# Summing the modulation products over column tiles and turning them on TensorE

## The reference, cut to what matters

```python
def _modulation(cond, w, b):
    m = jax.nn.silu(cond) @ w + b
    return jnp.split(m, 3, axis=-1)

for i in range(DEPTH):                      # DEPTH = 4
    shift, scale, gate = _modulation(c, ada_w[i], ada_b[i])
    hx = _rmsnorm(x, norm_g[i]) * (1.0 + scale[:, None]) + shift[:, None]
    if kind == 1 or update_ctx:             # layers 0 and 1: the context stream too
        cshift, cscale, cgate = _modulation(c_ctx, ada_w[i], ada_b[i])
    ...                                     # pool, neighbourhood attention, conv, pool mixer
    x = x + gate[:, None] * yx
```

## Time and profile before

| | |
|---|---|
| median of 3 runs | 1907.27 us (1906.62 to 1909.27) |
| the profiled execution | 1906.62 us, of which the traced span is 1904.7 us |
| PE busy | 1881.4 us, 99% of the span |
| PEld, DVE, ACT, POOL busy | 82%, 31%, 48%, 72% |
| granted TensorE clock, mean | 0.999 of full speed |

### The profile page before, as it was taken

The page is one execution under the profiler, slowest core; times in us unless marked ns, Lnnn a source line. Parts: engine busy times, 40 slices in busy tenths (PEclk is TensorE's granted clock), DMA queues, the critical chain, the costliest instruction groups (busy, mean ns, idle before and its releaser), DMA issues.

```text
span 1904.7 us, 27387 instructions
## 1 busy us (share of the span) xinstructions
PE 1881.4 (99%) x10810; PEld 1560.1 (82%) x10810; DVE 590.6 (31%) x1037; ACT 912.2 (48%) x1365; POOL 1362.3 (72%) x568
## 2 busy tenths in 40 slices
PE   6999999999999999999999999999999999999999
PEld 5888788887888888888788888888888878888887
DVE  4213522774652500235621400120022563041011
ACT  3224511765454643465554454454435555545442
POOL 2514443457777698878678898879887957898875
PEclk9999999999999999999999999999999999999999
DMA  9762675439748476556456566557655655556653
GB/s 359 250 218 67 205 256 196 120 104 310 268 159 298 152 233 194 177 178 184 136 161 189 176 198 190 179 164 238 201 177 167 192 150 155 187 157 211 195 178 121
DMA packets 194845, 364.09 MB, mean 191 GB/s; under 512 B 32260, under 2 KB 48372, under 8 KB 194164
## 3 DMA queue, kind: packets, MB, share of 16 engines
q1 hardware_dynamic: 191280, 351.72, 58.7%
q10 hardware_dynamic: 3460, 10.88, 1.7%
HBM read 361.50 MB, written 6.10 MB: 193 GB/s over the span
## 4 chain that ended last, share of the span: by engine, by line
PE 94%; DMA 3%; SPq 1%; ACT 1%; DVE 1%; ACTq 0%; issue 0%
PE ps L1140 27%; PE ps L1142 26%; PE ps L1141 26%; PE ps L1346 3%; DMA proj<-in_ada_w 2%; PE ps L1158 2%; PE ps L1820 1%; PE ps L1819 1%; PE ps L1818 1%; PE ps L1734 1%; PE ps L1178 1%; PE ps L1498 1%; PE ps L1469 1%; PE ps L1479 1%; PE ps L1779 1%; SPq L375 1%
## 5 line engine op out<-in xcount | busy, mean ns | idle before, releaser
L514 POOL TENSOR_TENSOR w_lo<-raw,w_hi 128x1024 fp32r<-128x1024 f32 x556 | 1343.4, 2450 | 496.8 <-ACT w_hi L552 496.6
L1140 PE MATMUL ps<-w_hi,xt_hi 128*128 128x512 f32 (+1 forms) x1952 | 759.3, 389 | 4.6 <-DVE xt_lo L1973 4.2
L1142 PE MATMUL ps<-w_hi,xt_lo 128*128 128x512 f32 (+1 forms) x1952 | 744.4, 381 | 0.0
L1141 PE MATMUL ps<-w_lo,xt_hi 128*128 128x512 f32 (+1 forms) x1952 | 743.8, 381 | 0.0
L552 ACT ACTIVATE w_hi<-raw 128x1024 fp32r<-128x1024 f32 x556 | 567.4, 1057 | 330.8 <-DMA raw<-in_ffn_w_up 98.8
L1140 PEld LDWEIGHTS ps<-w_hi,xt_hi 128*128 128x128 f32 x1952 | 367.6, 188 | 81.9 <-issue 12.5
L1142 PEld LDWEIGHTS ps<-w_hi,xt_lo 128*128 128x128 f32 x1952 | 367.3, 188 | 71.7
L1141 PEld LDWEIGHTS ps<-w_lo,xt_hi 128*128 128x128 f32 x1952 | 368.0, 189 | 65.7
L1140 PE MATMUL ps<-w_hi,xt_hi_ctx 128*128 128x512 f32 (+1 forms) x432 | 169.0, 391 | 0.2
L1142 PE MATMUL ps<-w_hi,xt_lo_ctx 128*128 128x512 f32 (+1 forms) x432 | 166.8, 386 | 0.0
L1141 PE MATMUL ps<-w_lo,xt_hi_ctx 128*128 128x512 f32 (+1 forms) x432 | 166.5, 385 | 0.0
(11 more groups left out here) (221 smaller groups left out, 1477.7 us busy)
## 6 DMA issues: line engine op xcount, KB each, us to landing
raw<-in_w_in SPq DMA_DIRECT2D x120, 512.0 KB, 3.7
raw<-in_ffn_w_gate SPq DMA_DIRECT2D x88, 512.0 KB, 3.8
raw<-in_ffn_w_up SPq DMA_DIRECT2D x88, 512.0 KB, 3.8
raw<-in_ffn_w_down SPq DMA_DIRECT2D x88, 512.0 KB, 3.5
pt<-in_ada_w SPq DMA_DIRECT2D x44, 512.0 KB, 5.8
raw<-in_pool_w_in SPq DMA_DIRECT2D x32, 512.0 KB, 8.3
raw<-in_na_w_in SPq DMA_DIRECT2D x32, 512.0 KB, 5.0
raw<-in_conv_w_in SPq DMA_DIRECT2D x32, 512.0 KB, 5.7
```

The costliest lines, as they stand in the source:

```text
L514: pool.tensor_tensor(w_lo[:, s, :], raw[:, s, :], w_hi[:, s, :].bitcast(F32), ALU.subtract).then_inc(lo_done, 1)
L1140: pe.matmul(o, h, hi, start=start, stop=False)
L1141: pe.matmul(o, h, lo, start=False, stop=False)
L1142: return pe.matmul(o, c, hi, start=False, stop=stop)
```

## The change

A matmul of the modulation now takes all 512 columns of a chunk at once. Chunk m writes partitions 32·(m % 4) to 32·(m % 4)+31 of the bank, so chunks 0 and 4 are added in the first column tile, 1 and 5 in the second, and so on: a piece is 8 matmuls of 512 columns where it was 32 of 128, and its bank holds four partial sums. DVE copies the whole bank to `ada_rows` (in `qt`) and signals `ada_copied`; PE transposes it in four 128x128 blocks back into the same bank (`ada_turn`, `ada_turned`); DVE adds the four partial sums with a reduction (`ada_sums`, `ada_summed`) and then the bias as before.

```diff
-        def ada_cols(a, dims):
-            return free(qt[:, 0:1, 0:1], dims, 16 * SEQ + (a % 2) * P)
+        ada_rows = free(qt[:, 0:1, 0:1], [[1, 512]], 16 * SEQ)
...
                     for c in range(2):
                         m = 2 * k + c
-                        for j in range(4):
-                            last = pe.matmul(ps[32 * j:32 * j + 32, bank, 0:P], cond[:, m, :],
-                                             free(ada_slot(k, a), [[P, 4], [1, 32]], c * 512 + 32 * j), start=m == 0, stop=m == KC - 1)
+                        p0 = (m % 4) * 32
+                        last = pe.matmul(ps[p0:p0 + 32, bank, :], cond[:, m, :], ada_slot(k, a)[:, c * 512:(c + 1) * 512],
+                                         start=m < 4, stop=m >= 4)
                     last.then_inc(ada_used, 1)
+            def ada_turn(a, bank):
+                pe.wait_ge(ada_copied, a + 1)
+                for q in range(4):
+                    last = pe.transpose(ps[:, bank, q * P:(q + 1) * P], ada_rows[:, q * P:(q + 1) * P], ident[:])
+                last.then_inc(ada_turned, 1)
...                                   # in one_block, ahead of the matmuls of tile t in group k
+                        late = len(tiles) == NT and k < 3
+                        if t == tiles[len(tiles) // 2]:
+                            if k in ada and not late:
+                                ada_turn(ada[k], bank)
+                            if k - 1 in ada and len(tiles) == NT:
+                                ada_turn(ada[k - 1], bank)
...                                   # in start()
                 ada_products(0, 0)
                 ada_products(1, 1)
+                ada_turn(0, 0)
                 turn_half(0, 0)
                 turn_half(1, 0)
+                ada_turn(1, 1)
                 pe.wait_ge(ada_read, 2)
...
                 part(1, 0)
+                ada_turn(2, 2)
                 part(1, 1)
                 ada_products(3, 3)
                 read_out(bank_of(0, 2))
                 part(2, 0)
+                ada_turn(3, 3)
                 part(2, 1)
...
             def ada_block(a, bank):
+                ada_copy(a, bank)
+                ada_sum(a, bank)
+
+            def ada_copy(a, bank):
+                dve.wait_ge(ada_used, 4 * a + 4)
+                dve.tensor_copy(ada_rows, ps[:, bank, :]).then_inc(ada_copied, 1)
+
+            def ada_sum(a, bank):
                 n, to = conditions(a), 4 * ADA_ORDER[a]
-                dve.wait_ge(ada_used, 4 * a + 4)
-                if a > 1:
-                    dve.wait_ge(ada_read, a - 1)
-                dve.transpose(ada_cols(a, [[1, P]]), ps[:, bank, 0:P]).then_inc(ada_turned, 1)
                 dve.wait_ge(ada_turned, a + 1)
-                dve.tensor_tensor(mods[:, to:to + 4, 0:n], ada_cols(a, [[32, 4], [1, n]]),
+                dve.tensor_reduce(ada_sums[:, :, 0:n], free(ps[:, bank, 0:1], [[P, 4], [1, n], [32, 4]]), AX.X,
+                                  ALU.add).then_inc(ada_summed, 1)
+                dve.wait_ge(ada_summed, a + 1)
+                dve.tensor_tensor(mods[:, to:to + 4, 0:n], ada_sums[:, :, 0:n],
                                   free(cols[:, 0:1], [[1, 4], [0, n]], C_ADAB + to), ALU.add).then_inc(ada_read, 1)
```

More of the change, by code:

```diff
@@ L192, in program @@
         cond = sb("cond", [P, KC, 32])
+        ada_sums = sb("ada_sums", [P, 4, 2])
         rope = sb("rope", [P, 2, NT, HD])
@@ L212, in program @@
         ada_in = [[sem(f"ada_in{u}{k}") for k in range(4)] for u in range(2)]
-        ada_used, ada_turned, ada_read = sem("ada_used"), sem("ada_turned"), sem("ada_read")
+        ada_used, ada_copied, ada_turned, ada_summed, ada_read = (
+            sem(x) for x in ("ada_used", "ada_copied", "ada_turned", "ada_summed", "ada_read"))
         hi_done = sem("hi_done")
@@ L2618, in _ @@
             normed("p0", 3)
-            ada_block(2, 2)
+            ada_copy(2, 2)
             full_units("p0", 2, (0,), *modulated(0))
+            ada_sum(2, 2)
             low_of_tile("p0", 2, 0, 4)
             full_units("p0", 3, (0,), *modulated(0))
-            ada_block(3, 3)
+            ada_copy(3, 3)
             low_of_tile("p0", 3, 0, 4)
+            ada_sum(3, 3)
             first_gains(1)
```

## The result

| | before | after |
|---|---|---|
| median | 1907.07 us of 4 runs (1906.62 to 1909.27) | 1918.85 us of 4 runs (1918.16 to 1920.13) |
| span of the profiled execution | 1904.7 us | 1916.1 us |

The ratio is 1.0062, with a 95% interval of 1.0049 to 1.0076: slower by 11.8 us. The forecast was 1918.0 us. The two profiles differ by 11.4 us. First the head of the page, part 1 for PE, and then PE's waits (us in total, times, longest), which answer to the earlier trace rows.

What follows compares the result with a forecast made beforehand. PE's stream was taken as the bound, busy 1881.4 of 1904.7 us. Terms 0 + 8.8 + 0.2 + 0.5 + 1.3 = 10.8 us on 1906.62 gave 1917.4, predicted as 1918.0 us; own range 1915 to 1922.5, 8-in-10 range 1914 to 1932.

Steps and rivals of the forecast that it cites:

- Products, 0: Modulation products on PE: 16 passes of 512 columns cost the same as 64 of 128, four tiles fully overlapping; 0 us.
- The partial overlap: Rival for the products: tiles overlap as if three of four worked, 0.6 us more a piece, 1932 us; chance 0.06.
- Turn, 20·0.44 = 8.8: Four transposes on PE for each of pieces 4 to 23, 0.44 us each with nothing hiding them; 8.8 us.
- Waits at k = 3, 0.2: Next block waits for DVE's sum and bias add behind the turn, in seven pieces; 0.2 us in all, between 0 and 2.8.
- at piece 21, 0.5: PE reaches the turn at 527.3 but DVE, busy with L2250, lets it go on at about 527.8; new wait of 0.5 us.
- Opening, 1.3: Kernel start: two matmuls of piece 2's last slice 0.44 us longer, plus two turns of 0.44; 1.3 us, 0.4 to 2.7.
- the anchor: Opening: the first large matmul's 1.2 us delay does not last, because PE waits at 30.50 for piece 2's last slice.
- Late slices, cancelling: Where a slice is late, the wait shrinks by up to 0.44 us and the last slice takes longer; taken to cancel.

Runs made afterwards that it cites:

- e10: The kernel before the change with the slices of pieces 19 and 20 issued one weight group earlier; 1906.85 us, ratio 0.9999.
- e6: The changed kernel with 24 idle transposes keeping PE busy before the first large matmul; 1918.74 us, ratio 1.0063.
- e7: The changed kernel without POOL's first wait (L523) and with 24 idle transposes on PE before the first large matmul; 1922.15 us, ratio 1.0079.
- e3: The changed kernel with neighbouring chunks on one column tile (chunk m in tile m // 2 instead of m % 4); 1922.75 us, ratio 1.0083.
- e8: The changed kernel with neighbouring chunks on one column tile, and slices of pieces 19 and 20 issued one weight group earlier; 1922.05 us, ratio 1.0079.
- e5: The changed kernel without POOL's first wait for DVE's first gains (L523); 1923.01 us, ratio 1.008.

## Why the prediction was right

The profiled span grew by 11.4 us, where the sum was 10.8.

- **Products, 0.** Right, to 0.014 us a piece. The net cost is 2.06 for 2.08 us in the trace, and the experiments without a turn and with one alone agree. The partial overlap is refuted here, where the four tiles had plain fp32 matmuls: the rule of the Trainium skill, "TensorE: Matmul & The Clock Gate", section "Measured speedup vs the span model", of 2.38 for three tiles at 512 columns, would have put the net cost at about 2.5, an estimate. Four groups of 0.43 us for sixteen passes are four tiles without loss.
- **Turn, 20·0.44 = 8.8.** Right in kind, small by a ninth: 20·0.493 = 9.9, because of the slower steps behind each. That is the term of the main cost that was mis-sized.
- **Waits at k = 3, 0.2, and at piece 21, 0.5.** Neither came. At piece 21 DVE is free and waits for PE: in the kernel before it was held by L2250 until 527.03, 4 us behind the products. The same line is L2277 now; it ends 1.5 us later than before, while the products come 10 us later (531.24 for 521.21). The chain of DVE work that ends with it begins at this line, before:

```profile
493.22 1.22 DVE L2228 TENSOR_TENSOR proj<-proj,ps 128x1024 f32<-128x1024 f32 x1 [7.84 <-PE ps L1142]
```

  and after, with its end and the copy:

```profile
503.23 1.22 DVE L2255 TENSOR_TENSOR proj<-proj,ps 128x1024 f32<-128x1024 f32 x1 [3.24 <-PE ps L1142]
...
527.34 1.23 DVE L2277 TENSOR_TENSOR proj<-proj 128x1024 f32<-128x1024 f32 x1
533.25 0.69 DVE L1915 COPY qt<-ps 128x512 f32<-128x512 f32 x1 [4.68 <-PE ps L1158]
```

  So the chain began 10.0 us later, just as PE's stream did, and it was right to set DVE's time from before against PE's time from before. What changed is its length: 25.3 us for 33.9 (493.22 to 527.10). The time of its instructions depends on what POOL does beside them: four of L2241 took 8.40 us from 498.04 in the kernel before, and four of the same line, L2268 now, 1.80 us from 522.90 and from 525.51 in the kernel after, while POOL stood still from 522.4 to 527.96. This length is not a property of the change: it is 25.3 us in e10, which has the code of the kernel before, and 31.1 in e6 and 33.3 in e7, which have the stream of the kernel after. With 33.9 us the copy would have ended at 537.8 and PE, which is at the turn at about 537.4, would have waited some 0.4 us. That the term came out at nothing is luck.
- **Opening, 1.3.** Too small: it is 2.4 us at the large matmul that started at 43.28 before and at 45.68 after. The parts: 1.4 at the start of piece 2 (28.81 to 30.21), −0.4 because its last slice is no longer late, two turns with what follows them 1.0, and 0.4 in a new wait for `xt_lo`:

```profile
40.51 0.87 DVE L1924 TENSOR_TENSOR mods<-ada_sums,cols 128x8 f32<-128x8 f32 x1
41.42 2.38 DVE L1946 SCALAR_TENSOR_TENSOR gains<-mods,cols 128x4 f32<-128x4 f32 x2
...
45.68 0.47 PE L1140 MATMUL ps<-w_hi,xt_hi 128*128 128x512 f32 x1 [0.41 <-DVE xt_lo L2000]
```

  The turn moved DVE's small instructions beside POOL's `w_lo`, where the gains take 2.38 us; before, they took 0.23 at 37.90, and POOL began at 38.33. The step that failed is the anchor: the delay of 1.2 us was to be swallowed by the late slice of piece 2 at 30.50. The slice swallowed 0.4, since by then PE was 1.4 late, more than the lateness of the slice. That the first large matmul came at 25.64 where I had 25.7 is luck: DVE's chain was 0.55 us shorter than I had it, and POOL's `w_lo`, which I had not counted, was ready later than `xt_lo`. The opening also swings from one execution to the next: e3 and e8 have the same code there, and piece 4 starts 0.4 us later than in the kernel after in the one and 2.1 us later in the other.
- **Late slices, cancelling.** They gave 0.9 back. Beyond the opening the kernel before loses 1.10, 0.42 and 0.31 us at pieces 7, 10 and 19, the kernel after 0.04 and 0.89 at pieces 7 and 10. A part of this is luck: the same stream loses 2.6 us in the trace of e6 and 3.8 in that of e5, and with these the slices would have cost 0.8 or 2.0 us instead of giving 0.9 back.

With what was measured the sum is 2.4 + 9.9 − 0.9 = 11.4 us, which is the difference of the spans. The mechanism and the main term are right; that the total is within 1 us is in part luck. The forecast's 10.8 hides an opening 1.1 too small and turns 1.1 too cheap against 0.7 of waits that never came and 0.9 that slices gave back.

## What to carry to other kernels

When PE is the bound, ask whether a rearrangement saves columns or only instructions: here a quarter of the instructions with the same columns saved nothing, and the extra work on PE, four transposes to bring partial sums together, was paid in full and some 10% more for the slower steps behind it. Read such a cost from the distance over many periods, not from the rows beside one. Take the length of a DVE chain that runs beside POOL as a range over several traces, not as a number from one: the same one took 25 to 34 us here. And when a delay is to be absorbed at a later anchor, compare the two lengths before counting on it: a wait swallows at most its own length.

## What the runs showed of the hardware that was not expected

- Column tiles are fed past a busy one: in e3 the first matmul of the last slice, seventh of eight in the program, starts 0.04 us behind the first, and 0.42 us ahead of that one's second pass.
- Behind the four transposes of a turn some ten large matmuls take 0.231 us on average and not 0.227. Behind the old products only four are slower, behind the new ones nearly ten.
- A DVE instruction on eight values a partition took 1.53 us, and two on four values took 2.33, beside POOL instructions of 2.3 us; each ended within 0.1 us of POOL's.
- The landing of a 512 KB slice swings enough to move the end of the whole kernel: the pieces that met a late slice cost 0.9 us in the profiled execution of the kernel after, 2.6 in that of e6 and 3.8 in that of e5, whose streams behind the opening are the same. Why the slices of piece 19 are later in some of them was not found.
